# One wide matmul in place of six transposes between two units of an FFN, in a two-model transformer kernel on one core

## The chip, the cores and the metric

The kernel runs on one core of one Trainium2 chip. The metric is the device time of one execution in microseconds, and the median of several executions is what two versions are compared by. Lower is better.

## The reference, cut to what matters

Two transformer models run one after the other on 256 tokens of width 1024, two layers each. The first has in each layer a SwiGLU FFN, a mixer (dilated and stick-breaking attention with gates) and a second SwiGLU FFN. The second has in each layer a mixer with four branches and one FFN with a short convolution. So there are six FFNs, each with 2816 hidden columns:

```python
def swiglu(x, w_gate, w_up, w_down):
    return (jax.nn.silu(x @ w_gate) * (x @ w_up)) @ w_down

# first model, for each layer l
x = x + 0.5 * swiglu(rms_norm(x, norm_ffn1[l]), ffn1_w_gate[l], ffn1_w_up[l], ffn1_w_down[l])
x = x + hybrid_mixer(rms_norm(x, norm_mix[l]), ...)
x = x + 0.5 * swiglu(rms_norm(x, norm_ffn2[l]), ffn2_w_gate[l], ffn2_w_up[l], ffn2_w_down[l])

# second model, for each layer l
u = causal_depthwise_conv(hf @ ffn_w_up[l], ffn_conv_w[l], ffn_conv_b[l])
gate, val = jnp.split(u, 2, axis=-1)
f = (jax.nn.gelu(gate, approximate=True) * val) @ ffn_w_down[l]
```

## The kernel before, in words

**Numbers.** Every large product is computed from float32 operands split in two: a high part (`whi`, `hhi`, `hidhi`) and a low part (`wlo`, `hlo`, `hidlo`), both of type float32r. One product of a 128 x 128 weight block with 128 x 256 activations is three matmuls (`mm3`, lines 615 to 617): high by high, high by low, low by high. Smaller products (rotations, sums, transposes) are plain float32.

**Weights.** All weights stream through a ring of three slots of 1 MB (`raw`). SyncE loads a slot, ScalarE rounds it to the high part (L1288), VectorE subtracts to get the low part (L1824) and raises `lo_ready[slot]`, and TensorE waits for that in `unit_ready`. One such load is called a unit. A unit is 48 matmuls of 256 columns on TensorE.

**An FFN.** `ffn` (line 721) is called six times by TensorE. The hidden columns are taken in 11 pairs of blocks (`PAIRS`). `start()` enters the FFN: it takes the first gate unit and the first up unit while the normalized activations still arrive. Then the loop over `p` from 1 to 10 takes three units a turn: a gate unit in slot 2 (`column_block(2, ...)`), an up unit in slot 0, and a down unit in slot 1 for the pair before (`down`), which accumulates into the four PSUM banks 4 to 7 (`acc`). A last down unit ends the FFN. The order is fixed by hand; waits stand only on semaphores of the slots and of the activations.

**The place of the change.** At `p == 2` in each FFN, and once more at `p == 7` of the very first (`PAR_PAIR + 2`, two turns after `turn_par` has transposed the parameter rows), the kernel waits for the gate unit in slot 2 and then calls `turns_between` (line 627). It issues six transposes of 128 x 128 blocks of `xT`, the residual stream, into a PSUM bank. Nobody reads what they write: the bank is 2 in the first model and 3 in the second (`5 - odd`), and the next gate block that uses the bank starts a new accumulation. So there are seven calls in an execution. The matmul ahead of each is the last of a down unit, the one behind it the first of a gate unit.

**Other matmuls named below.** L672 (`widened`) multiplies `ones` with a 256-column float32 tile. L875 and L1050 multiply a rotation table with 512 columns of float32. L1055 is four float32 matmuls of 256 columns in a row. A plain float32 matmul stands in the trace as two records.

Of the kernel before, what the change touches and what calls it, by code (L numbers as in the profile page):

```python
# [12 lines left out]
P = 128  # L13
# [182 lines left out]
def hybrid_network(nc, A, ident_in, c1_in, c2_in, out):  # L196


    with ExitStack() as ctx:
        def sb(name, cols, dt=F32):  # L200
            return ctx.enter_context(nc.sbuf_tensor(name, [P, cols], dt))[:, :]
# [7 lines left out]
        def view(buf, **dims):  # L209

            names = " ".join(dims)
            return buf.rearrange(f"p ({names}) -> p {names}", **dims)
# [12 lines left out]
        xT = view(sb("xT", KC * SEQ), c=KC, t=SEQ)  # L225
# [8 lines left out]
        ident = sb("ident", P)  # L234
        neg_ones = sb("neg_ones", P)
        zero_col = sb("zero_col", 1)
        ones = sb("ones", P)
# [136 lines left out]
        def bank(b, a=0, n=512):  # L374
            return ps[:, b, a:a + n]
# [134 lines left out]
        def gate_bank(p, odd):  # L510

            return odd if p % 2 else 0
# [99 lines left out]
        def _(pe):  # L612
            def mm3(o, w_hi, w_lo, m_hi, m_lo, start, stop):

                pe.matmul(o, w_hi, m_hi, start=start, stop=False, skip_group_check=True)  # L615
                pe.matmul(o, w_hi, m_lo, start=False, stop=False, skip_group_check=True)  # L616
                return pe.matmul(o, w_lo, m_hi, start=False, stop=stop, skip_group_check=True)  # L617

            def unit_ready(slot, uses):
                pe.wait_ge(lo_ready[slot], uses + 1)  # L620
# [3 lines left out]
                for _ in range(n):  # L624
                    pe.matmul(bank(0), zeros[:, 0:P], zeros[:, :], start=True, stop=True, skip_group_check=True)

            def turns_between(b):

                for n in range(6):
                    pe.transpose(bank(b, (n % 4) * P, P), xT[:, n, 0:P], ident)  # L630

            def enter(units, h_base, lag, after_k, after, first=False):

# [41 lines left out]
            def post_sums(m, b):  # L675

                for c in (2 * b, 2 * b + 1):
                    last = column_sums(post_event(m), b, post_sq, c, c == 0, c == KC - 1)
                last.then_inc(col_sum, 1)
# [9 lines left out]
            def project(slot, half, o):  # L689

                for k in range(KC):
                    c = k * UC + half * P
                    last = mm3(o, whi[:, slot, c:c + P], wlo[:, slot, c:c + P], hhi[:, k, :], hlo[:, k, :],
                               k == 0, k == KC - 1)
                return last
# [13 lines left out]
            def acc(c):  # L709

                return bank(4 + c // 2, (c % 2) * SEQ, SEQ)
# [9 lines left out]
            def ffn(uses, f, start, odd, m=None):  # L721

                fp = f * PAIRS

                def column_block(slot, u, b):
                    unit_ready(slot, u)
                    project(slot, 0, bank(b, 0, SEQ))
                    project(slot, 1, bank(b, SEQ, SEQ)).then_inc(used[slot], 1)

                def down(slot, u, buf, first, final):  # L730
                    unit_ready(slot, u)
                    for c in range(KC):
                        for i in range(2):
                            w = slice(i * D + c * P, i * D + (c + 1) * P)
                            last = mm3(acc(c), whi[:, slot, w], wlo[:, slot, w], hidhi[:, buf, i, :], hidlo[:, buf, i, :],
                                       first and i == 0 and c % 2 == 0, final and i == 1)
                        if final and c % 2 and c < KC - 1:
                            last.then_inc(acc_done, 1)
                        if final and m is not None and c % 2 and c > 1:
                            if c == KC - 1:  # L740
                                last.then_inc(used[slot], 1)
                            post_sums(m, c // 2 - 1)
                    if not final or m is None:
                        last.then_inc(used[slot], 1)

                start()
                for p in range(1, PAIRS):
                    if p >= 2:
                        pe.wait_ge(gate_taken, fp + p - 1)
                    if f == 0 and p == 1:  # L750
                        pe.wait_ge(first_kept, 1)
                    if f == 0 and p == PAR_PAIR + 2:
                        pe.wait_ge(par_ready, len(PAR_TILES))
                    if p == 2 or f == 0 and p == PAR_PAIR + 2:
                        unit_ready(2, uses(0) + p - 1)
                        turns_between(5 - odd)
                    column_block(2, uses(0) + p - 1, gate_bank(p, odd))
                    pe.wait_ge(up_taken, fp + p)
                    column_block(0, uses(0) + p, 1)
                    pe.wait_ge(hid_ready, fp + p)  # L760
                    if f == 0 and p == 1:
                        pe.wait_ge(x_updated, KC)
                    if f == 0 and p == PAR_PAIR:
                        turn_par()
                    down(1, uses(0) + p, (p - 1) % 2, p == 1, False)
                pe.wait_ge(hid_ready, fp + PAIRS)
                down(2, uses(0) + PAIRS - 1, 0, False, True)

            def turn_par():

                pe.wait_ge(par_in, 16 * n_par)
                for i, n in enumerate(PAR_TILES[1:]):
                    if i == 4:
                        pe.wait_ge(gate_taken, PAR_PAIR + 1)
                    last = pe.transpose(bank(2 + i // 4, (i % 4) * P, n), parrow[0:n, i + 1, :], ident[0:n, 0:n])
                    if i % 4 == 3:
                        last.then_inc(par_turned, 1)
# [67 lines left out]
            for t, done in ((0, x_in_0), (1, x_in_1)):  # L845
# [5 lines left out]
                if t == 0:  # L851
                    n = PAR_TILES[0]
# [168 lines left out]
            for l in range(0, DEPTH):  # L1021
                u0, u1 = (lambda s: uses1(l, s)), (lambda s: uses1(l, FFN_UNITS + M1_END + s))
                ffn(u0, 2 * l, lambda: plain_start(((0, u0(0)), (1, u0(0))), 3 * l, l == 0), 3)
                mixer1(l)
                ffn(u1, 2 * l + 1, lambda: plain_start(((0, u1(0)), (1, u1(0))), 3 * l + 2), 3)
# [238 lines left out]
            for l in range(0, DEPTH):  # L1264
                mixer2(l)
                u2 = lambda s: uses2(l, M2_END + s)
                ffn(u2, 2 * DEPTH + l, lambda: pre_start(2 * l, ((0, u2(0)), (1, u2(0))), 3 * DEPTH + 1 + 2 * l), 2, 2 * l + 1)
                post_end(2 * l + 1)
# [1330 lines left out]
```

## Time and profile before

| | before |
|---|---|
| median of 3 runs | 2200.01 us (2197.58, 2200.01, 2208.09) |
| the profiled execution's own time | 2200.01 us |
| span of that execution (first to last instruction) | 2198.2 us |
| time outside the span | 1.8 us |
| TensorE busy | 2134.4 us, 97% of the span |
| VectorE, ScalarE, GpSimd busy | 1496.4, 1100.4, 126.9 us |
| mean granted TensorE clock | 0.989 of full speed |

The busy time of TensorE is a union of intervals that overlap: a matmul of 256 columns is shown with a length of about 0.28 us, but the next one starts 0.11 to 0.12 us after it. The distance from one start to the next, here called the pitch, says how fast the engine goes. The view of windows gives the number of instructions in a stretch in brackets; at a pitch of 0.12 us, two that had begun before the stretch are still running in it and are counted too.

### The profile page before, as it was taken

How to read it: one execution, taken by the hardware profiler on the slowest of the kernel's cores; microseconds unless marked ns; L12 is line 12 of the kernel's file. 1: busy time of each engine (PE TensorE's matmuls, PEld its weight loads, DVE VectorE, ACT ScalarE, POOL GpSimd, SP SyncE). 2: the span in 40 equal slices, each digit the busy share in tenths (PEclk: the TensorE clock that was granted, in tenths of full speed). 3: DMA queues.
4: the chain of work that ended last, by engine and by line, in shares of the span. 5: the costliest groups of instructions: out<-in, count | busy, mean ns of one | idle time of the engine just before them, and what ended most of it. 6: DMA issues, size and time to landing. Idle time of an engine off the chain costs nothing.

```text
span 2198.2 us, 40932 instructions
## 1 busy us (share of the span) xinstructions
PE 2134.4 (97%) x17994; PEld 2059.5 (94%) x17994; DVE 1496.4 (68%) x1814; ACT 1100.4 (50%) x1336; POOL 126.9 (6%) x116
## 2 busy tenths in 40 slices
PE   8999999999999999999999799999999989999998
PEld 8999999999999999999999698999999879899998
DVE  5556757555655775755568996667766899666775
ACT  5445365544544546544442667455554265655554
POOL 0001000100100100000000000001000000001100
PEclk9999999999999999999999899999999989999999
DMA  7555544565566553565553454346554344444652
GB/s 260 180 187 172 172 145 163 177 203 195 174 194 196 177 163 126 165 208 192 192 182 117 135 156 134 133 154 211 192 179 137 117 138 151 135 156 142 202 192 77
DMA packets 285044, 367.26 MB, mean 167 GB/s; under 512 B 10002, under 2 KB 257730, under 8 KB 284610
## 3 DMA queue, kind: packets, MB, share of 16 engines
q1 hardware_dynamic: 281138, 361.01, 50.6%
q10 hardware_dynamic: 3728, 3.62, 0.5%
q8 instruction: 142, 2.33, 0.4%
q14 instruction: 36, 0.29, 0.0%
HBM read 363.56 MB, written 1.05 MB: 166 GB/s over the span
## 4 chain that ended last, share of the span: by engine, by line
PE 85%; DVE 9%; ACT 3%; issue 1%; DMA 1%; POOL 0%; ACTq 0%; SPq 0%; DVEq 0%
PE ps L615 25%; PE ps L616 24%; PE ps L617 24%; DVE wlo L1824 2%; ACT whi L1288 2%; PE ps L703 1%; PE ps L705 1%; PE ps L704 1%; PE ps L664 1%; DVE sq L2437 1%; PE ps L1055 1%; PE ps L1072 1%; PE ps L1082 1%; PE ps L1103 1%; DVE arena L2113 0%
## 5 line engine op out<-in xcount | busy, mean ns | idle before, releaser
L615 PE MATMUL ps<-hhi,whi 128*128 128x256 f32 x3808 | 1079.7, 284 | 18.0 <-DVE hlo L1830 7.3
L1824 DVE TENSOR_TENSOR wlo<-raw,whi 128x2048 fp32r<-128x2048 f32 (+1 forms) x347 | 781.6, 2254 | 418.2 <-ACT whi L1288 418.1
L616 PE MATMUL ps<-hlo,whi 128*128 128x256 f32 x3808 | 1057.4, 278 | 0.0
L617 PE MATMUL ps<-hhi,wlo 128*128 128x256 f32 x3808 | 1057.3, 278 | 0.0
L1288 ACT ACTIVATE whi<-raw 128x2048 fp32r<-128x2048 f32 (+1 forms) x347 | 653.5, 1886 | 681.9 <-PE ps L617 596.0
L615 PEld LDWEIGHTS ps<-hhi,whi 128*128 128x128 f32 x3808 | 717.2, 188 | 35.2 <-issue 11.2
L616 PEld LDWEIGHTS ps<-hlo,whi 128*128 128x128 f32 x3808 | 716.5, 188 | 4.8 <-issue 4.3
L617 PEld LDWEIGHTS ps<-hhi,wlo 128*128 128x128 f32 x3808 | 716.0, 188 | 0.2
L615 PE MATMUL ps<-hidhi,whi 128*128 128x256 f32 x1056 | 292.9, 277 | 0.7 <-DVE hidlo L2194 0.7
L617 PE MATMUL ps<-hidhi,wlo 128*128 128x256 f32 x1056 | 292.1, 277 | 0.0
L616 PE MATMUL ps<-hidlo,whi 128*128 128x256 f32 x1056 | 292.1, 277 | 0.0
L615 PEld LDWEIGHTS ps<-hidhi,whi 128*128 128x128 f32 x1056 | 198.6, 188 | 1.3 <-DVE hidlo L2194 1.1
L616 PEld LDWEIGHTS ps<-hidlo,whi 128*128 128x128 f32 x1056 | 198.4, 188 | 0.0
L617 PEld LDWEIGHTS ps<-hidhi,wlo 128*128 128x128 f32 x1056 | 198.2, 188 | 0.0
L1366 ACT ACTIVATE arena<-arena 128x512 f32<-128x512 f32 x44 | 27.8, 633 | 171.5 <-DVE arena L1859 171.5
L615 PE MATMUL ps<-brhi,whi 128*128 128x256 f32 x320 | 92.1, 288 | 7.5 <-DVE brlo L2545 6.7
L2437 DVE SCALAR_TENSOR_TENSOR sq<-arena,par,sq 128x256 f32<-128x256 f32 x240 | 98.1, 476 | 0.0
L1781 POOL TENSOR_TENSOR arena<-arena,rstd 128x512 f32<-128x512 f32 x44 | 57.0, 1296 | 618.2 <-ACT arena L1366 592.7
L616 PE MATMUL ps<-brlo,whi 128*128 128x256 f32 x320 | 90.4, 283 | 0.0
L617 PE MATMUL ps<-brhi,wlo 128*128 128x256 f32 x320 | 90.4, 282 | 0.0
L2189 DVE SCALAR_TENSOR_TENSOR arena<-arena,par 128x256 f32<-128x256 f32 x176 | 73.5, 478 | 1.5 <-ACT arena L1550 1.3
L615 PEld LDWEIGHTS ps<-brhi,whi 128*128 128x128 f32 x320 | 62.1, 194 | 9.3 <-issue 7.7
(288 smaller groups left out, 2105.6 us busy)
## 6 DMA issues: line engine op xcount, KB each, us to landing
raw<-in_ffn_w_up SPq DMA_DIRECT2D x88, 1024.0 KB, 5.3
raw<-in_w_in SPq DMA_DIRECT2D x68, 1024.0 KB, 5.2
raw<-in_ffn_w_down SPq DMA_DIRECT2D x66, 1024.0 KB, 4.8
raw<-in_ffn_w_gate SPq DMA_DIRECT2D x43, 1024.0 KB, 5.3
raw<-in_w_gate SPq DMA_DIRECT2D x32, 1024.0 KB, 5.3
raw<-in_w_branch SPq DMA_DIRECT2D x16, 1024.0 KB, 4.9
raw<-in_nsa_cmp_w SPq DMA_DIRECT2D x8, 1024.0 KB, 5.5
raw<-in_w_out SPq DMA_DIRECT2D x6, 1024.0 KB, 4.9
```

Source lines behind the costliest of these rows:

```text
L615: pe.matmul(o, w_hi, m_hi, start=start, stop=False, skip_group_check=True)
L616: pe.matmul(o, w_hi, m_lo, start=False, stop=False, skip_group_check=True)
L617: return pe.matmul(o, w_lo, m_hi, start=False, stop=stop, skip_group_check=True)
L664: last = pe.matmul(bank(2, n * t, n), src[:, chunk, t * P:(t + 1) * P], w, start=first and t == 0, stop=final, skip_group_check=True)
L703: pe.matmul(o[:, t, :], hhi[:, k, tok], whi[:, slot, c:c + n], start=(k == 0), stop=False)
L704: pe.matmul(o[:, t, :], hlo[:, k, tok], whi[:, slot, c:c + n], start=False, stop=False)
L1288: act.activation(whi[:, slot, 0:n], raw[:, slot, 0:n], ACT.Copy).then_inc(hi_ready[slot], 1)
L1366: act.activation(act_out, gate_sb, ACT.Silu).then_inc(act_done, 1)
L1781: pool.tensor_tensor(scaled.rearrange("p (c t) -> p c t", c=2), act_out.rearrange("p (c t) -> p c t", c=2), rstd_over(2), ALU.mult).then_i ...
L1824: dve.tensor_tensor(wlo[:, slot, 0:n], raw[:, slot, 0:n], whi[:, slot, 0:n].bitcast(F32), ALU.subtract) \
L2189: dve.scalar_tensor_tensor(conv2[:, w, c, :], pad2[:, w, c, tap:tap + SEQ], par_col(ch + tap * FCH), conv2[:, w, c, :], ALU.mult, ALU.add) ...
L2437: dve.scalar_tensor_tensor(conv_acc[:, c, :], x, w, conv_acc[:, c, :], ALU.mult, ALU.add) \
```

## The change

`turns_between` goes, and `wide_between` takes its place at the same seven points: one float32 matmul of the constant tile `ones` (128 x 128, as weights) with the first two chunks of `xT` (512 columns), into the whole of the same bank. Its result is not read either.

```diff
-            def turns_between(b):
-
-                for n in range(6):
-                    pe.transpose(bank(b, (n % 4) * P, P), xT[:, n, 0:P], ident)
+            def wide_between(b):
+
+                pe.matmul(bank(b), ones, xT[:, 0:2, :], start=True, stop=True, skip_group_check=True)
...
                     if p == 2 or f == 0 and p == PAR_PAIR + 2:
                         unit_ready(2, uses(0) + p - 1)
-                        turns_between(5 - odd)
+                        wide_between(5 - odd)
                     column_block(2, uses(0) + p - 1, gate_bank(p, odd))
```

## Rows read from the trace of the kernel before

**Rows 1.** Page: busy time by engine, and the granted clock in 40 slices

```profile
PE 2134.4 (97%) x17994; PEld 2059.5 (94%) x17994; DVE 1496.4 (68%) x1814; ACT 1100.4 (50%) x1336; POOL 126.9 (6%) x116
...
PEclk9999999999999999999999899999999989999999
```

**Rows 2.** Page: the chain that ended last, by engine

```profile
PE 85%; DVE 9%; ACT 3%; issue 1%; DMA 1%; POOL 0%; ACTq 0%; SPq 0%; DVEq 0%
```

**Rows 3.** Waits of TensorE, longest in total: us, times, longest

```profile
PE ps L1164 <- DVE gates L2423: 17.1, 2, 8.8
```

**Rows 4.** Groups of TensorE by shape: records, busy us, mean ns, idle before

```profile
L1055 PE MATMUL ps<-arena,consts 128*128 128x256 f32 x64 | 15.4, 384 | 0.0
L875 PE MATMUL ps<-arena,consts 128*128 128x512 f32 x24 | 12.3, 592 | 0.0
L1050 PE MATMUL ps<-arena,consts 128*128 128x512 f32 x16 | 8.2, 597 | 1.5 <-DVE arena L2292 1.5
L630 PE MATMUL ps<-ident,xT 128*128 128x128 f32 x42 | 5.7, 272 | 0.0
L672 PE MATMUL ps<-ssum,ones 128*128 128x256 f32 x16 | 5.3, 411 | 0.5
```

**Rows 5.** Windows: stretch, length, TensorE busy (instructions), clock, DMA share, GB/s

```profile
45.06:107.13 62.07, 62.07 (x529) 1.00 0.56 185
131.26:201.70 70.44, 70.44 (x624) 1.00 0.59 193
398.18:409.37 11.19, 11.19 (x96) 1.00 0.72 240
410.15:562.20 152.05, 152.05 (x1344) 1.00 0.61 196
593.20:745.00 151.80, 151.80 (x1342) 1.00 0.60 197
941.20:951.98 10.78, 10.78 (x96) 1.00 0.71 233
1486.20:1632.80 146.60, 146.60 (x1296) 1.00 0.61 198
2028.90:2175.50 146.60, 146.60 (x1296) 1.00 0.54 177
```

**Rows 6.** Timeline of TensorE about the first call: start, us, line

```profile
44.28 0.82 PE L630 MATMUL ps<-ident,xT 128*128 128x128 f32 x6
...
45.06 0.28 PE L616 MATMUL ps<-hlo,whi 128*128 128x256 f32 x1
```

**Rows 7.** Timeline of TensorE about a 512-column float32 matmul

```profile
221.32 1.02 PE L875 MATMUL ps<-arena,consts 128*128 128x512 f32 x2
...
222.30 0.28 PE L616 MATMUL ps<-hlo,whi 128*128 128x256 f32 x1
```

**Rows 8.** Windows behind L875, and ahead of and behind L672

```profile
222.30:227.64 5.34, 5.34 (x49) 1.00 0.65 213
2008.74:2010.74 2.00, 2.00 (x18) 1.00 0.69 232
2011.29:2022.36 11.07, 11.07 (x96) 1.00 0.39 121
```

**Rows 9.** Timeline of TensorE about four float32 matmuls at L1055

```profile
1726.27 0.28 PE L617 MATMUL ps<-hhi,wlo 128*128 128x256 f32 x1
...
1731.22 0.28 PE L617 MATMUL ps<-hhi,wlo 128*128 128x256 f32 x1
...
1731.69 1.89 PE L1055 MATMUL ps<-arena,consts 128*128 128x256 f32 x8
...
1734.00 0.28 PE L617 MATMUL ps<-hhi,wlo 128*128 128x256 f32 x1
...
1738.76 0.28 PE L617 MATMUL ps<-hhi,wlo 128*128 128x256 f32 x1
```

## The prediction

> **What bounds the kernel now.** I read the page first. TensorE is busy 97% of the span and no other engine reaches 70% [rows 1]; the chain that ended last lies 85% on TensorE [rows 2]. The waits of TensorE add up to some 60 us, the largest 17.1 us in the second model's mixers [rows 3], and none of them lies in the body of an FFN: from the `p == 2` call to the last down unit the windows show TensorE busy for their whole length [rows 5]. So every nanosecond that TensorE spends at the seven calls, or per matmul behind them, goes straight into the time. The granted clock is 1.00 in all these windows [rows 5], so the clock gate is not what differs between them.
>
> The pitch is. I divided the length of each window by its count less two. From 45.06 us, behind the first call, 62.07 us hold 527 matmuls: 117.8 ns each. From 131.26 us, behind the call at `p == 7`, 70.44 us hold 622: 113.3 ns. The other FFNs behind their calls give 152.05/1342 = 113.3, 151.80/1340 = 113.3 and twice 146.60/1294 = 113.3 ns [rows 5]. It is the same loop with the same shapes at the same clock, and it has two paces, slow and fast, 4.5 ns apart (4%). A pace, once there, lasts for hundreds of matmuls; it changes only where something else comes between them.
>
> Then I looked at what comes between. Ahead of the call in the second FFN, 11.19 us hold 94 matmuls: 119 ns, slow within the count's error of one; behind it the pace is fast. Ahead of the call in the fourth, 10.78/94 = 114.7, fast within that error [rows 5]; the third and the two FFNs of the second model are like it. So the seven calls are: slow to slow at 44 us, slow to fast at 130 and 409 us, fast to fast four times. The six transposes ended the slow pace two times in three and never ended the fast one.
>
> **The change part by part.**
>
> *The instructions.* From the first transpose to the second matmul of the gate unit is 45.06 - 44.28 = 0.78 us [rows 6]. The trace has the new matmul's shape, 128 x 512 float32 with a constant table as weights, at L875 and L1050 [rows 4]: from its first record to the same place behind it is 222.30 - 221.32 = 0.98 us [rows 7]. The difference is 0.20 us a call, and seven calls give +1.4 us. Both ends are measured the same way, and nothing hides either. `xT`, `ones` and the bank are free at that point as they were for the transposes, so no wait is added; SyncE, ScalarE and VectorE lose or gain nothing.
>
> *The pace behind a fast stretch.* A 512-column float32 matmul between fast matmuls leaves them fast: behind the one at 221.32 us, 5.34/47 = 113.6 ns [rows 8], and the same at all eight places of L875 and seven of L1050 where such matmuls lie on both sides without a wait. So the four fast-to-fast calls cost only the 0.20 us.
>
> *The pace behind a slow stretch.* The trace has no 512-column float32 matmul in a slow stretch, so this is bounded from both sides. The nearest row in form is L672: one float32 matmul, two records, weights and moving operand of float32. It came at 2010.74 us in a slow stretch, 2.00/16 = 125 ns by a short window whose error is one in 16 and 117.8 by its starts, and behind it the pace stayed slow: 11.07/94 = 117.8 ns [rows 8]. That happened in three of three cases of a lone 256-column float32 matmul. The other bound is L1055: four such matmuls, eight records. Ahead of them 42 matmuls took 1731.22 - 1726.27 = 4.95 us, 117.9 ns; behind them 42 took 4.76 us, 113.3 ns [rows 9]. So enough float32 work does end the slow pace. The wide matmul has two records like L672, but each twice as long. I take it to be like L672, since the number of records is what sets L672 apart from L1055 most, and leave 1 in 3 for the other.
>
> *What that costs.* With the wide matmul slow stays slow. The first call changes nothing (slow before, slow after). The call at 130 us no longer ends the slow pace: 622 matmuls x 4.5 ns = 2.8 us. Nor does the one in the second FFN: 1342 x 4.5 ns = 6.0 us. The low bound of both is zero, or below for the first FFN (next part).
>
> *Sum.* 1.4 + 2.8 + 6.0 = 10.2 us. The profiled execution took 2200.0 us, which is also the median, so the sum gives **2210.2 us**, +0.46%. A measurement here can tell 0.5%, 11.0 us, from no change, so this is just inside.
>
> [...]
>
> **The rivals.**
>
> *A. The wide matmul ends the slow pace* as L1055 does [rows 9]. Then the calls at 130 and 409 us do what they did, and the first call may do better: if the pace turns fast at 45 us, 527 matmuls up to `turn_par` save 527 x 4.5 = 2.4 us, and the 191 from there to the second call may save 0.9 more. The sum is between +1.4 and 1.4 - 3.3 = -1.9 us: 2198.1 to 2201.4 us. Against it stands L672, for it that its records are half as long.
>
> *B. The wide matmul leaves the slow pace, and more FFNs enter slow.* This is the rival on the other side of the bound. The pace with which an FFN is entered is set at a wait of TensorE, where the matmuls start again when VectorE delivers; that was slow for two FFNs of six (the first and the second) and fast for four [rows 5]. Every such start comes at another instant once the work ahead is shifted, so it may come out otherwise. The transposes made that harmless; a matmul that preserves the pace lets it last for the whole FFN. Each further slow FFN costs 1294 to 1342 x 4.5 = 5.8 to 6.0 us: 2216.2 with one more, 2222 with two. It decides from the first one on, since 10.2 + 5.8 is over 11.0 us. The spread of the three runs of before, 10.5 us, shows that something of this size varies between executions.
>
> *C. The wide matmul leaves the slow pace, and the second FFN happens to enter fast.* Then only the first FFN's stretch is lost: 1.4 + 2.8 = 4.2 us, 2204.2 us.
>
> *D. The pace is not set at the calls at all*, but by something that merely coincides. Then only the instructions count, 2201.4 us. Against it: the pace changes at 131 and 410 us exactly behind the transposes, and nowhere else inside a loop.
>
> **How the numbers follow.** The forecast 0.27, A 0.33, B 0.27, C 0.10, D 0.03. That the wide matmul leaves the slow pace is the likeliest mechanism (forecast, B and C: 0.64), and its middle case is the forecast, with a range of its own from 2204 to 2216 us. The mixers' paces are drawn anew as well and move each case by up to 2 us. The range holds 8 in 10 from 2197.5 us (the low end of A, less a little) to 2217.5 us (B with one more slow FFN, and a little); B with two or more is left out above, and a luckier A below. Slower by over 0.5% (above 2211.0 us) is B and a good third of the forecast's own spread: 0.36. Faster by over 0.5% would need 11 us, and the whole of A's gain is 2: 0.03. Within 0.5% is the rest: 0.61.
>
> **What the profile of the changed kernel would show.** From the wide matmul's first record to the second matmul of the gate unit 0.98 us, seven times. The window behind the first call at 117.8 ns; at 113.3 ns it is A. The windows from the call at 130 us to 202 us and through the second FFN at 117.8 ns, some 2.8 and 6.0 us longer for the same count; other FFNs at 113.3 ns, or at 117.8 where TensorE came in slow (B). In each FFN the pace behind the call should be the pace ahead of it: a single change from slow to fast across a wide matmul speaks for A. No new wait of TensorE at the calls, and clock 1.00 there. The prediction is wrong above all if a slow pace ends at the wide matmul, or if the pace at the entries of the later FFNs comes out otherwise than in this execution.

## The result, and the profile after

The kernel with the wide matmul takes 2219.83 us (median of 6 runs, 2217.87 to 2227.51), the kernel before 2200.39 us (median of 6, 2197.58 to 2208.09). The ratio is 1.0089, 95% interval 1.0067 to 1.0110: slower by 0.9%, clear of noise and of the 0.5% bound. The forecast was 2210.2 us with a range up to 2217.5, so the measured time lies above the range. (The kernel before was measured again with each batch of experiments below, and its median moved between 2200.4 and 2208.1 us; each ratio there is against the kernel before of its own batch.)

The profiled execution of the changed kernel took 2222.2 us, with a span of 2220.4 us against 2198.2 before. The page, and the longest wait of TensorE, hardly differ from [rows 1] and [rows 3]:

```profile
PE 2159.3 (97%) x17966; PEld 2079.9 (94%) x17966; DVE 1497.8 (67%) x1814; ACT 1099.7 (50%) x1336; POOL 127.1 (6%) x116
...
PEclk9999999999999999999999899999999989999999
```

The first row of the waits of TensorE (us in total, times, longest):

```profile
PE ps L1163 <- DVE gates L2422: 16.9, 2, 8.7
```

TensorE is 24.9 us longer busy, with the same work but for the seven calls. The other engines' times moved by 1.4 us at most, and the rows of TensorE's waits add up to 55 us against 58 before (no single row grew by more than 0.3 us). The place to look is the windows. These answer to [rows 5], the columns are the same, and the pitch is again the length over the count less two. They come by pairs, a stretch ahead of a wide matmul and the body of the FFN behind it; the third row, alone, is behind the second call:

```profile
24.50:43.90 19.40, 19.40 (x171) 1.00 0.77 268
44.90:104.60 59.70, 59.70 (x529) 1.00 0.57 192
128.97:199.00 70.03, 70.03 (x597) 1.00 0.56 188
...
398.50:409.60 11.10, 11.10 (x96) 1.00 0.74 245
410.67:568.70 158.03, 158.03 (x1344) 1.00 0.57 187
588.50:599.30 10.80, 10.80 (x94) 1.00 0.73 254
600.31:758.20 157.89, 157.89 (x1343) 1.00 0.56 187
955.60:966.30 10.70, 10.70 (x96) 1.00 0.73 245
967.30:1119.30 152.00, 152.00 (x1344) 1.00 0.60 200
...
2034.00:2044.90 10.90, 10.90 (x93) 1.00 0.36 125
2045.93:2192.50 146.57, 146.57 (x1247) 1.00 0.52 176
```

Divided: first FFN 59.70/527 = 113.3 ns, and behind its second call 70.03/595 = 117.7; second 158.03/1342 = 117.8; third 157.89/1341 = 117.7; fourth 152.00/1342 = 113.3; last 146.57/1245 = 117.7. Three bodies run at the slow pace that all ran fast in [rows 5], at the same granted clock of 1.00. The short stretches ahead say the same pace each time (19.40/169 = 114.8, 11.10/94 = 118.1, 10.80/92 = 117.4, 10.70/94 = 113.8, 10.90/91 = 119.8; a short stretch can be off by one or two counts, and by the starts of the matmuls the five are 113.3, 117.8, 117.8, 113.3 and 117.8).

The timeline about the third call, start, length, line, answers to [rows 6]:

```profile
409.70 1.02 PE L629 MATMUL ps<-xT,ones 128*128 128x512 f32 x2
...
410.67 0.28 PE L616 MATMUL ps<-hlo,whi 128*128 128x256 f32 x1
```

From the first record to the second matmul of the gate unit is 0.97 us. With each call's start in both traces the 22.2 us can be laid out by stage:

| start of | before | after | later by | gained in the stage |
|---|---|---|---|---|
| 1st call | 44.28 | 43.93 | -0.35 | -0.35 |
| 2nd call | 130.49 | 127.99 | -2.50 | -2.15 |
| 3rd call (second FFN) | 409.37 | 409.70 | 0.33 | +2.83 |
| 4th call (third FFN) | 592.40 | 599.33 | 6.93 | +6.60 |
| 5th call (fourth FFN) | 951.98 | 966.32 | 14.34 | +7.41 |
| 6th call (fifth FFN) | 1485.42 | 1501.80 | 16.38 | +2.04 |
| 7th call (sixth FFN) | 2028.11 | 2044.96 | 16.85 | +0.47 |
| end of the span | 2198.2 | 2220.4 | 22.2 | +5.35 |

Three slow bodies give 6.0 + 6.0 + 5.8 = 17.8 us, the lost reset at the second call 2.8, the calls 1.4, and the first FFN, which was fast from its entry this time, returns 2.4 + 0.35. That is 19.2 us. The remaining 3 us lie in the mixers and at the entries: the slow pace of the third FFN outlived its end. In the mixer behind it, 12 us held 96 records in the kernel before (from 771.0 us) and 94 in the same work of the changed one (from 784.5 us), and that stage lost 1.2 us beside the body and the call.

### The profile page after: what moved, and what is told of

It is laid out like the page before. It is cut to its first block, busy times and chain, and to the rows that moved or that the text cites. A ratio compares the mean times of both kernels' runs of the same rounds, so it can differ in the third digit from the quotient of the medians.

```text
span 2220.4 us, 40876 instructions
## 1 busy us (share of the span) xinstructions
PE 2159.3 (97%) x17966; PEld 2079.9 (94%) x17966; DVE 1497.8 (67%) x1814; ACT 1099.7 (50%) x1336; POOL 127.1 (6%) x116
## 4 chain that ended last, share of the span: by engine, by line
PE 86%; DVE 9%; ACT 3%; issue 1%; DMA 1%; POOL 0%; ACTq 0%; SPq 0%; DVEq 0%
PE ps L615 25%; PE ps L617 25%; PE ps L616 25%; DVE wlo L1823 2%; ACT whi L1287 2%; PE ps L702 1%; PE ps L703 1%; PE ps L704 1%; PE ps L663 1%; DVE sq L2436 1%; PE ps L1054 1%; PE ps L1071 1%; PE ps L1102 1%; PE ps L1081 1%; DVE arena L2112 0%
```

## The experiments

In the counts below a pace is "slow" (117.8 ns) or "fast" (113.3 ns), taken from the starts of the matmuls of lines 615 to 617 ahead of and behind a call in the profiled execution. Each kernel has seven calls, so each profile shows seven passages.

### Nothing at the seven points

```diff
-                        turns_between(5 - odd)
```

> Nothing stands at the seven points. Pace theory (a slow pace of 117.8 ns or a fast one of 113.3 ns is set where TensorE restarts after a wait, and goes on until something ends it): the instructions save 7 x 0.66 = 4.6 us, and in every FFN the pace behind the point is the pace ahead of it, in seven of seven; with three or four slow stretches, as in the changed kernel, some 2196 + 6 for each slow FFN, 2208 to 2220 us. Rival, instructions: the wide matmul itself costs the 20 us, by its length or by what it does to the weight loads behind it; then without it and without the transposes the time is 2195 to 2196 us and no slow pace is left behind the points.

Measured: 2202.3 us (10 runs, 2196.2 to 2211.2) against 2207.0 (14 runs, 2199.6 to 2211.5), ratio 0.999 [0.9972, 1.0008]. Not to be told apart from the kernel before. The profiled execution has a span of 2197.2 us, and slow stretches that run on, one in the first FFN behind `turn_par` (95.60/812 = 117.7 ns) and one through the whole fifth FFN (157.00/1333 = 117.8), beside fast ones (second FFN 162.00/1430 = 113.3). At all seven points, now empty, the pace went on as it was:

```profile
104.60:200.20 95.60, 95.60 (x814) 1.00 0.58 188
397.00:559.00 162.00, 162.00 (x1432) 1.00 0.63 202
1478.00:1635.00 157.00, 157.00 (x1335) 1.00 0.58 191
```

The rival "instructions" is half refuted: slow stretches are there without any filler. But only one of the five later bodies was slow, fewer than expected, and the time was below the range that the pace theory gave. The transposes cost 4.6 us, and the interval puts the kernel without them between 6.2 us below and 1.8 above the kernel before; so what they save in slow bodies lies between nothing and some 6 us.

### The wide matmul, then the six transposes

```diff
+                        wide_between(5 - odd)
                         turns_between(5 - odd)
```

> The wide matmul and behind it the six transposes, at all seven points. Pace theory: the transposes end the slow pace as before, so the bodies run at 113.3 ns and only the wide matmuls' own 0.85 us are added, seven times: 2200.4 + 6.0 = 2206 us, plus or minus 3 for the first FFN. Rival, instructions: whatever the wide matmul does stays, 2224 us or more.

Measured: 2215.5 us (5 runs) against 2207.0, ratio 1.0053 [1.0028, 1.0077]. That is +11.7 us, between the two expectations. The passages explain it: fast to fast four times, slow to fast twice, and slow to slow once, at the fourth call:

```profile
583.00:593.70 10.70, 10.70 (x93) 1.00 0.77 251
595.50:752.00 156.50, 156.50 (x1331) 1.00 0.57 188
```

156.50/1329 = 117.8 ns. One failed reset costs 6 us; with the 6.0 us of the seven wide matmuls that would make the 12 measured, by the passages of this one execution. So the wide matmul's effect is not something that stays, but the transposes are not a sure reset.

### Records or columns: two narrow matmuls, two wide ones

```diff
-                for n in range(6):
-                    pe.transpose(bank(b, (n % 4) * P, P), xT[:, n, 0:P], ident)
+                for n in range(2):
+                    pe.matmul(bank(b, (n % 2) * SEQ, SEQ), ones, xT[:, n % 2, :], start=True, stop=True, skip_group_check=True)
```

> Two float32 matmuls of 256 columns in place of one of 512: the same columns and the same length (0.86 us), but four records and four weight loads where the wide one has two. If the number of records counts (eight at L1055 ended the slow pace, two at L672 did not), slow paces end at the points in most cases and the time is near 2202 us. If the time spent in float32 work counts, it is like the wide one: pace behind equals pace ahead, 2212 to 2222 us.

```diff
-                pe.matmul(bank(b), ones, xT[:, 0:2, :], start=True, stop=True, skip_group_check=True)
+                for _ in range(2):
+                    pe.matmul(bank(b), ones, xT[:, 0:2, :], start=True, stop=True, skip_group_check=True)
```

(The second diff is against the changed kernel.)

> Two wide matmuls: four records, 1.71 us a call, 1.05 us more than the transposes before a pace is counted (+7.4 us in all over the kernel before). If records count, the slow paces end: about 2207 us. If time in float32 work counts, 1.7 us is half of what the eight records at L1055 took together plus as much again, the slow paces end too: 2207 us. If neither (only transposes end it, and L1055 was a chance), pace behind equals pace ahead: 2220 to 2228 us.

Measured: 2223.7 us (4 runs), ratio 1.0091 [1.0066, 1.0115], and 2230.3 us (4 runs), ratio 1.0119 [1.0095, 1.0144], both against 2207.0. The differences, +20 and +26 us, refute "the slow paces end" (+2 and +7). They lie within the slower expectations, which were written over 2200.4 us (+12 to +22, +20 to +28), but for another reason than those gave: the pace behind is not the pace ahead. The passages of the two kernels are alike, call by call: fast to slow four times, slow to fast twice, slow to slow once. The windows ahead of and behind the third and the fourth call of the kernel with two wide matmuls:

```profile
400.00:410.40 10.40, 10.40 (x95) 1.00 0.75 239
412.40:570.00 157.60, 157.60 (x1340) 1.00 0.58 187
590.00:600.90 10.90, 10.90 (x95) 1.00 0.72 243
602.90:754.00 151.10, 151.10 (x1335) 1.00 0.60 194
```

111.8 (fast, to one count) becomes 157.60/1338 = 117.8; 117.2 becomes 151.10/1333 = 113.4. So columns don't matter here and the number of records does (two narrow matmuls have the columns and the length of one wide one, 0.98 us to the second matmul behind, and act otherwise), but not by ending the slow pace: four records turned the pace into the other one in twelve passages of fourteen. My notion of float32 work that "relaxes" the slow pace into the fast one fell here.

### Is the entry pace the kernel's or the execution's?

> A second profile of the kernel before. If the pace with which each FFN is entered belongs to the kernel, the seven calls show the same paces ahead as in the first profile (slow, slow, slow, fast, fast, fast, fast), and slow to fast behind those at 130 and 409 us. If it is drawn anew in each execution, two or more of them differ, and the time differs by 6 us for each FFN that is slow behind its call.

> A second profile of the changed kernel. Pace theory: behind each of the seven wide matmuls the pace is the pace ahead of it, whatever it is there. If entries belong to the kernel, slow at the second, third, fourth and seventh call again, and 2217 to 2222 us; if they are drawn anew, other calls, and a time between 2202 us (none slow) and 2238 us (all).

Measured, one execution each: 2203.3 and 2220.4 us. The kernel before entered otherwise than in its first profile at four of seven calls: now fast, slow, fast, fast, fast, slow, slow. Behind all of them it was fast. The windows ahead of and behind its sixth call:

```profile
1475.00:1485.60 10.60, 10.60 (x91) 1.00 0.39 127
1486.50:1632.00 145.50, 145.50 (x1286) 1.00 0.60 199
```

10.60/89 = 119.1 (117.8 by the starts) becomes 145.50/1284 = 113.3 ns. The changed kernel showed the very same seven as in its first profile: fast, slow, slow, slow, fast, fast, slow, each kept by the wide matmul. So the pace at a call can differ between executions of one kernel, and in another kernel it repeated; why is open.

The two profiles of the changed kernel came to the same paces by different ways, though. In the second to fourth FFN, two units (96 matmuls) ahead of the `p == 2` call, TensorE waits for the low part of the first up unit of the loop (0.58 us in the first profile, up to 398.32 us). These are the stretches ahead of that wait in the second FFN, of the changed kernel's first and second profile:

```profile
390.60:397.40 6.80, 6.80 (x62) 1.00 0.46 150
...
390.30:397.60 7.30, 7.30 (x64) 1.00 0.43 141
```

6.80/60 = 113.3 and 7.30/62 = 117.7 ns: in the first profile the FFN came in fast and turned slow across the wait, in the second it was slow already. In the third FFN it was the other way round.

### Three and four narrow matmuls

The diff is that of two narrow matmuls, with `range(3)` and `range(4)`.

> Three float32 matmuls of 256 columns, six records, 1.29 us. Two records kept each pace, four turned it into the other one in six of seven calls, whether they were narrow or wide. If it goes by an even and odd number of matmuls, six records keep the pace; if more records end the slow pace only, slow turns into fast and fast stays. Keeping: 2210 to 2222 us. Ending: about 2206 us.

> Four float32 matmuls of 256 columns, eight records, 1.72 us, as at L1055, where slow turned fast and fast stayed fast. If that holds, all seven calls are fast behind, and the time is 2200.4 + 7 x 1.05 = 2208 us less some 3 us for the first FFN. If odd and even decide, the paces are switched as with two matmuls (fast to slow and slow to fast), 2220 us or more.

Measured against 2202.4: three, 2223.8 us (2 runs), ratio 1.0095 [1.0060, 1.0129]; four, 2212.5 us (8 runs, 2208.3 to 2215.6), ratio 1.0044 [1.0029, 1.0059]. Three: slow to fast three times, slow to slow once, fast to slow three times; neither "odd and even" nor "ends the slow pace" says this. Four: fast to fast four times, slow to fast twice, slow to slow once, near what L1055 did [rows 9], but not sure either (in the kernel before only two of the eight places of L1055 have a run of such matmuls right ahead of them, one slow and one fast). The kernel with four, behind its fourth and its second call:

```profile
598.20:749.00 150.80, 150.80 (x1333) 1.00 0.58 194
131.10:200.00 68.90, 68.90 (x587) 1.00 0.54 181
```

150.80/1331 = 113.3 ns; 68.90/585 = 117.8 ns.

### The transposes kept in the first FFN alone

```diff
-                        wide_between(5 - odd)
+                        turns_between(5 - odd) if f == 0 else wide_between(5 - odd)
```

(Against the changed kernel.)

> The transposes stay at the two calls of the first FFN, the wide matmul stands at the five others. Direct cost 5 x 0.20 = 1.0 us. Two theories of the entry pace. Carried: the second and third FFN enter slow in the changed kernel because the first FFN ends slow; with the transposes it ends fast, they enter fast, and the time is near 2201 to 2208 us. Drawn at the restart: the second FFN and later ones enter slow or fast as it comes, each slow one stays slow behind the wide matmul at 6 us, 2207 to 2220 us. In both, pace behind equals pace ahead at the five wide calls, and slow turns fast at the second call.

Measured: 2212.8 us (8 runs, 2206.1 to 2218.3) against 2204.4, ratio 1.0042 [1.0026, 1.0058]. In the profiled execution the second and third FFN entered and stayed fast, the fourth, fifth and sixth entered and stayed slow. The fourth:

```profile
939.00:949.80 10.80, 10.80 (x94) 1.00 0.76 249
950.90:1103.00 152.10, 152.10 (x1294) 1.00 0.59 188
```

10.80/92 = 117.4 and 152.10/1292 = 117.7 ns. In the changed kernel the same FFN was fast in both profiles, and the second and third slow. So a slow entry is not simply carried over from a slow FFN ahead (the slow pace of the fourth FFN began at a wait two units ahead of the call, and the third had been fast); and where the wide matmul stands, five passages of five keep the pace.

### One transpose, twelve, and the six placed elsewhere

```diff
-                for n in range(6):
+                for n in range(1):
```

The other kernel has `range(12)` there and takes `xT[:, n % KC, 0:P]`.

> One transpose in place of six, at all seven calls: 5 x 0.108 = 0.54 us less a call, 3.8 us in all. If it is the transpose's form behind float32r matmuls that ends the slow pace, one does it too, and the time is 2200.4 - 3.8 = 2197 us. If it takes the run of six, a single one keeps or switches the pace, and slow bodies come back at 6 us each: 2203 to 2215 us.

> Twelve transposes: 0.65 us more a call, 4.5 us in all. If the transposes bring weight loads and matmuls step by step to the phase of the fast pace, twelve never fail, where six failed once in six slow calls: all seven fast behind, 2205 us less up to 3 for the first FFN. If a phase merely maps onto another, twelve fail as often as six.

Measured against 2204.4: one transpose, 2210.8 us (5 runs, 2201.1 to 2213.2), ratio 1.0032 [1.0014, 1.0050]; twelve, 2218.6 us (2 runs), ratio 1.0069 [1.0049, 1.0090]. One turned slow into fast four times in five and kept fast twice. Twelve, expected to be the surest, turned fast into slow twice, kept slow once. Ahead of and behind its third call:

```profile
401.00:411.30 10.30, 10.30 (x93) 1.00 0.75 243
412.90:568.00 155.10, 155.10 (x1319) 1.00 0.59 189
```

10.30/91 = 113.2 becomes 155.10/1317 = 117.8 ns. That fells the idea of a gradual approach for transposes too, by one profiled execution.

```diff
-                        turns_between(5 - odd)
...
                     pe.wait_ge(up_taken, fp + p)
+                    if p == 1 or f == 0 and p == PAR_PAIR + 1:
+                        unit_ready(0, uses(0) + p)
+                        turns_between(1)
```

That is, the six transposes (of `ident`, since `xT` is still being written) go ahead of the first up unit in each FFN, and one turn sooner behind `turn_par`.

> The six transposes, of the constant identity into bank 1, stand ahead of the first up unit behind the entry (p == 1) in each FFN, and at p == 6 of the first FFN: same number and cost as in the kernel before, but 96 matmuls sooner behind each entry and 96 behind turn_par. Pace theory: they still turn slow into fast, and a slow entry costs 96 x 4.5 = 0.43 us less, so 1 to 2 us below the kernel before, 2199 to 2203 us where that has 2200 to 2204: not to be told apart. Rival, that it is what follows that counts (the transposes only work ahead of the gate unit of p == 2): slow bodies stay slow, 2206 to 2220 us.

Measured: 2208.3 us (12 runs, 2201.3 to 2221.0) against 2208.1 (17 runs, 2197.1 to 2213.9), ratio 1.0004 [0.9984, 1.0024]: the same time. But two of seven passages turned fast into slow, the first and the last, which the six transposes at `p == 2` never did. Its last FFN:

```profile
2010.00:2020.50 10.50, 10.50 (x93) 1.00 0.53 168
2021.50:2170.00 148.50, 148.50 (x1263) 1.00 0.56 185
```

10.50/91 = 115.4, which by the starts is 113.3, becomes 148.50/1261 = 117.8 ns. The place is not all that changed: the bank and the transposed operand did too, so which of them did it isn't shown. No kernel here beats the kernel before by more than its measurement can tell.

### All passages together

| between the paces | profiles | slow to fast | slow to slow | fast to fast | fast to slow |
|---|---|---|---|---|---|
| one wide matmul | 3 | 0 | 11 | 8 | 0 |
| six transposes at `p == 2` | 3 | 6 | 1 | 9 | 0 |
| wide matmul and six transposes | 1 | 2 | 1 | 4 | 0 |
| two matmuls, narrow or wide | 2 | 4 | 2 | 0 | 8 |
| three narrow | 1 | 3 | 1 | 0 | 3 |
| four narrow | 1 | 2 | 1 | 4 | 0 |
| one transpose | 1 | 4 | 1 | 2 | 0 |
| twelve transposes | 1 | 1 | 1 | 3 | 2 |
| six transposes two units sooner | 1 | 3 | 0 | 2 | 2 |

Does the pace account for the times? Of the regular matmuls of lines 615 to 617 (by a mean of nine pitches in a row), 19% ran slow in the kernel before, 52% in the changed one, 64% with two narrow ones. For each of the fourteen profiled executions, sum what the pitch from one such matmul to the next has over 113.3 ns (pitches up to 125 ns, so that waits stay out). That is 15.2 us in the kernel before, 35.9 in the changed one and 42.9 with two narrow ones. Take from the span this sum, the span times one less the mean granted clock, and the seven calls at their own length (4.6 us before, 6.0 changed). The spans lie between 2197.2 and 2228.5 us; what remains lies between 2148.5 and 2153.5 us. So the spread of 31 us shrinks to 5; in the changed kernel against the kernel before, 20.7 of the 22.2 us are the pace by this count.

## Why the prediction was right and wrong, point by point

**TensorE bounds, no wait is added, the clock is not it: right.** The same waits (55 us in the rows against 58), the same 1.00 in every body.

**The instructions, +1.4 us: right.** The wide call takes 0.97 to 0.98 us in each of seven, the transposes took 0.77 to 0.78.

**Fast stays fast behind the wide matmul: right,** 8 of 8 in three profiles.

**Slow stays slow behind it: right,** 11 of 11. I had given this 0.64, on three cases of L672; read again, only two of them (1468.05 and 2010.74 us) had the slow pace ahead, the third (1667.06 us) kept a fast one, so the ground was thinner than the prediction says. Rival A, that it ends the slow pace, did not come about in a single passage. The reason I gave, that the number of records and not their length decides, is borne out by the two kernels with four records, narrow and wide, whose passages are alike, one profile of each. But what I took more records to do, to end the slow pace, is wrong: four mostly switch the paces. That came from one slow case of L1055.

**The second call, +2.8 us: right.** The pace ahead of it was slow in all twelve profiles with a call there, behind `turn_par`, and the stage shows +2.83 us.

**The first call, no change: wrong in this case and small.** The first FFN entered fast, which returned 2.5 us net. Its entry varies too: slow in the first profile of the kernel before, fast in the second.

**How many later FFNs enter slow: this step failed.** I read the entry paces off one execution, took the likeliest number of slow bodies among the last five to be the one that it showed, and left two further ones outside the range. The runs show that another execution can come out otherwise. Over the twelve profiles with a call at `p == 2`, 25 of 60 such entries were slow, and two executions of the kernel before differ at four of seven calls. At 25 of 60, five FFNs with bodies of 5.9 us give 12 us in the mean, not 6; the changed kernel has three slow in both its profiles, 17.8 us. That is rival B with two further slow bodies, for which the text had 2222 us against 2222.2 us of the profiled execution, and which the range cut off at 2217.5. That the two numbers meet so closely is luck: the first FFN gave 2.75 us back and 3 us came up in mixers and entries, and B had neither. That a kept slow pace costs a whole body was the forecast's and B's alike; the mis-sized term is "1342 x 4.5 ns = 6.0 us", one body, which measured 17.8 us, three.

**How the pace at a call comes about: wrong for the most part.** The text has it set at a wait of TensorE where the FFN starts. The traces of the same twelve profiles show two other ways. In the second to fourth FFN the last wait ahead of the call (0.3 to 0.6 us) left the pace as it was in 30 of 36 cases; it turned fast into slow five times and slow into fast once. In the fifth and sixth FFN all 24 came out of the entry slow, in the kernel before too (11.07/94 = 117.8 ns in [rows 8], a stretch of its sixth FFN), and what decided was the first matmul of the first down unit, ahead of which there is a pause of less than 0.2 us: behind it 13 were fast and 11 slow. The first row below is the sixth FFN of the kernel before in its first profile, behind that pause: fast. The other two are from its second profile, ahead of the pause and behind it, slow both times; the same 48 records take 5.34 and 5.50 us:

```profile
2022.76:2028.10 5.34, 5.34 (x48) 1.00 0.46 154
...
2014.41:2025.48 11.07, 11.07 (x96) 1.00 0.37 117
2025.90:2031.40 5.50, 5.50 (x48) 1.00 0.50 177
```

**The rest,** 3 us in mixers and entries against "up to 2": the slow pace crossed the end of a body, as it did into the mixer behind the third FFN.

**The Trainium skill** ("TensorE: Matmul & The Clock Gate", section "Back-to-back issue gap") gives N / 2.4 + 2.5 ns as the gap of an isolated matmul at full clock, by which 109.2 ns is an estimate for 256 columns. It says that in a stream of weight loads and matmuls both set the spacing, so that this formula counts too little at small N and too much at large N. The traces agree in so far as no body here ran at 109.2 ns. That such a stream has two paces, 113.3 and 117.8 ns, is what the runs add, and which of them it was made most of the 20 us.

**What stays open.** What the two paces are. All that the traces show is that a stream of alternating weight loads and matmuls stays in either of two pitches, and that what stands between two stretches maps one onto the other in a way that depends on the number of records, on the place (or on the bank and operand that changed with it), and on something in the slow pace that the starts don't show (one slow passage in seven went otherwise than the rest for six transposes). Each kernel but the first two was profiled once, so most rows of the table rest on seven passages. Why the changed kernel enters slow more often (three of five, twice alike) than the kernel before (one and two) was not settled. Luck alone is unlikely: if each of five entries were slow with 25 in 60 and on its own, three executions in ten would have at most one slow body among the five, two fewer than the profiled one's three and so near 2210 us, and none of the eight executions of the changed kernel lay below 2217.9 us (0.69 to the eighth power is 5 in 100). On the other hand its two profiles came to the same paces by different ways.

## What to carry to other kernels

When TensorE is saturated, compare the pitch of its matmuls between stretches of the same loop at the same granted clock: two stretches that differ by 4% here cost more than any wait, and a busy share of 100% hides it. An instruction that does nothing for the result may be there for what it does to the pace behind it, so before replacing it by one of similar length, look at the pace ahead of and behind every instance. And a state that can come out otherwise in another execution must be counted over several before its odds go into a forecast; one trace shows one case.

## What the runs showed of the hardware that was not expected

A float32r matmul stream of 128 x 128 weights and 256 columns has two stable pitches at the full clock of 2.4 GHz, 113.3 and 117.8 ns, each held for over 1300 matmuls. (This and what follows is what the traces of this kernel show; nothing here says how general it is.) One plain float32 matmul of 512 columns (two records, 0.98 us) kept either in 19 passages of 19. Two such matmuls, of 512 or of 256 columns, turned fast into slow in 8 of 8. Twelve transposes turned fast into slow in 2 of 5, where six at the same place did so in none of 9. The second to sixth FFN came slow to their call in 25 of 60 cases; waits of 0.3 to 0.6 us left the pace as it was in 30 of 36, and a pause of less than 0.2 us turned slow into fast in 13 of 24.
